# The end of a one-core decoder layer: feed-forward accumulators combined on VectorE in one block, and the residual added inside the output DMAs

## What is computed

```
mix = concat(latent_attention, sliding_window_attention) @ w_o
x1  = x + rms_norm(mix, g_mix_post)
h   = rms_norm(x1, g_ffn_pre)
ff  = (silu(h @ w_gate) * (h @ w_up)) @ w_down        # 2048 -> 5632 -> 2048
out = x1 + rms_norm(ff, g_ffn_post)
rms_norm(y, g) = y * rsqrt(mean(y*y) + 1e-6) * g
```

## Time and profile before

| | |
|---|---|
| median of 3 runs | 2082.83 us (2082.64 to 2082.87) |
| the profiled execution | 2083.53 us |
| its span in the trace | 2081.7 us |
| PE busy | 1998.4 us, 96% |
| DVE busy | 1114.0 us, 54% |
| ACT busy | 684.9 us, 33% |
| POOL busy | 113.6 us, 5% |
| granted PE clock, mean of the span | 0.986 of full speed |

### The profile page before, as it was taken

One profiled execution on the slowest core, in us unless ns is written; L12 is line 12 of the kernel. 1 busy time (PEld: TensorE's weight loads), 2 busy tenths in 40 slices (PEclk: granted clock), 3 DMA queues, 4 the chain that ended last, 5 costly groups with the idle time before them and its releaser, 6 DMA issues. The chain is left out here.

```text
span 2081.7 us, 21411 instructions
## 1 busy us (share of the span) xinstructions
PE 1998.4 (96%) x9062; PEld 1651.1 (79%) x9062; DVE 1114.0 (54%) x1278; ACT 684.9 (33%) x850; POOL 113.6 (5%) x64
## 2 busy tenths in 40 slices
PE   8999879999998999999999999999999999999994
PEld 6888667778886888888888888888888788888873
DVE  5753585563225433433334333343334788888887
ACT  5331463453226222222222222222222633333342
POOL 1200130000003000000000000000000000000034
PEclk9999999999998999999999999999999999999997
DMA  7433201115321554454444654445542756545633
GB/s 240 111 101 96 66 12 57 54 43 200 101 94 48 192 162 129 125 168 139 137 144 140 194 144 137 118 135 158 150 134 79 267 222 243 212 181 214 242 124 119
DMA packets 292058, 293.24 MB, mean 141 GB/s; under 512 B 4899, under 2 KB 228220, under 8 KB 286204
## 3 DMA queue, kind: packets, MB, share of 16 engines
q1 hardware_dynamic: 288928, 285.23, 43.1%
q10 hardware_dynamic: 3036, 6.66, 1.0%
HBM read 243.09 MB, written 51.93 MB: 142 GB/s over the span
## 5 line engine op out<-in xcount | busy, mean ns | idle before, releaser
L534 PE MATMUL pair<-act_hi,whi 128*128 128x512 f32 x1712 | 669.7, 391 | 0.0
L536 PE MATMUL pair<-act_hi,wlo 128*128 128x512 f32 x1712 | 666.5, 389 | 0.0
L535 PE MATMUL pair<-act_lo,whi 128*128 128x512 f32 x1712 | 666.3, 389 | 0.0
L425 DVE TENSOR_TENSOR wlo<-raw,whi 128x2048 fp32r<-128x2048 f32 x134 | 296.2, 2213 | 247.5 <-ACT whi L418 247.5
L534 PEld LDWEIGHTS pair<-act_hi,whi 128*128 128x128 f32 x1712 | 321.7, 188 | 67.0 <-issue 1.1
L536 PEld LDWEIGHTS pair<-act_hi,wlo 128*128 128x128 f32 x1712 | 321.5, 188 | 67.1
L535 PEld LDWEIGHTS pair<-act_lo,whi 128*128 128x128 f32 x1712 | 321.7, 188 | 66.1 <-issue 0.5
L418 ACT ACTIVATE whi<-raw 128x2048 fp32r<-128x2048 f32 x135 | 248.5, 1843 | 358.9 <-PE pair L536 338.3
L1979 PE MATMUL pair<-ring_hi,hfs 128*128 128x512 f32 x528 | 206.3, 391 | 4.6 <-DVE ring_lo L1500 4.6
L1981 PE MATMUL pair<-ring_hi,hfs 128*128 128x512 f32 x528 | 206.0, 390 | 0.0
L1980 PE MATMUL pair<-ring_lo,hfs 128*128 128x512 f32 x528 | 206.0, 390 | 0.0
(11 more groups left out here) (260 smaller groups left out, 2125.5 us busy)
## 6 DMA issues: line engine op xcount, KB each, us to landing
raw<-in_w_gate SPq DMA_DIRECT2D x44, 1024.0 KB, 5.5
raw<-in_w_up SPq DMA_DIRECT2D x44, 1024.0 KB, 5.7
w_b<-in_w_down SPq DMA_DIRECT2D x40, 1024.0 KB, 5.0
h_forms<-hst SPq DMA_DIRECT2D x22, 1792.0 KB, 7.3
hfs<-h_forms SPq DMA_DIRECT2D x30, 1024.0 KB, 7.7
raw<-in_w_in SPq DMA_DIRECT2D x19, 1024.0 KB, 5.7
raw<-in_w_o SPq DMA_DIRECT2D x16, 1024.0 KB, 4.9
xin<-in_x SPq DMA_DIRECT2D x4, 1024.0 KB, 11.2
```

The source lines that it names most:

```text
L425: last = nc.vector.tensor_tensor(dst, src, f(hi), ALU.subtract)
L534: nc.tensor.matmul(out_ap, a[0], b[0], start=first, stop=False)
L535: nc.tensor.matmul(out_ap, a[0], b[1], start=False, stop=False)
L536: return nc.tensor.matmul(out_ap, a[1], b[0], start=False, stop=last)
```

## The change

1. POOL's ten additions and DVE's four are gone from iterations 10 and 11. Instead DVE does all fourteen (`mix(0)`, `mix(1)`) directly behind the low part of P83, followed by the gain multiplications of cb 0, and only then the adds of P81 and P82.
2. x1 is written to the output tensor itself in place of `x1_dram`. It isn't read back.
3. y is scaled by rstd in place: by ACT for both halves of t = 0 and 1 and the right half of t = 3, by DVE (`y_normed`) for both halves of t = 2 and the left half of t = 3. POOL issues eight DMAs of 128 x 1024 that add y to what stands in the output (`accum_op=ALU.add`). SP issues no output DMA.
4. ACT's squares of iteration 10 move behind its last high part.

```diff
-                        sp_.dma_start(x1_dram[t], x1[:, t, :]).then_inc(x1_out, 16)
+                        sp_.dma_start(out_v[t], x1[:, t, :]).then_inc(x1_out, 16)
...
-                elif it + 1 == ITERS and f_ in (1, 3, 4, 5):
-                    sp_.wait_ge(d_lo, n + 1)
-                    t = (1, 3, 4, 5).index(f_)
-                    sp_.dma_start(x1_row[t][:, :], x1_dram[t]).then_inc(x1_in[t], 16)
...
-            for t in range(TB):
-                sp_.wait_ge(y_ready, t + 1)
-                w = shared(t).stop
-                sp_.dma_start(out_v[t][:, 0:1024], x1_row[t][:, 0:1024]).then_inc(y_out, 16)
...
-            sp_.wait_ge(y_out, 16 * (2 * TB + 1))
+            sp_.wait_ge(y_out, 16 * 2 * TB)
...
-            for it in (ITERS - 2, ITERS - 1):
-                cb = it % 2
-                before = 5 * (it - ITERS + 2)
-                pool.wait_ge(*evictions(7 * it))
-                add_into(5, 0, cb)
...
+            def add_to_out(t, half):
+                nc.gpsimd.dma_start(out_v[t][:, 1024 * half:1024 * half + 1024], y_part(t, half),
+                                    accum_op=ALU.add).then_inc(y_out, 16)
+
+            pool.wait_ge(x1_out, 16 * TB)
+            for t in (0, 1):
+                for half in (0, 1):
+                    pool.wait_ge(y_scaled, 2 * t + half + 1)
+                    add_to_out(t, half)
+            for half in (0, 1):
+                pool.wait_ge(y_ready, half + 1)
+                add_to_out(2, half)
+            pool.wait_ge(y_scaled, 5)
+            add_to_out(3, 1)
+            pool.wait_ge(y_ready, 3)
+            add_to_out(3, 0)
...
+                if n == PRODUCTS - 1:
+                    act.wait_ge(d_done, PRODUCTS - 7)
+                    for half, t0, done in ((0, 0, 1), (1, 0, 4), (0, 2, 6), (1, 2, 7)):
+                        act.wait_ge(y_mixed, done)
+                        y_square(t0, half, 0)
+                        y_square(t0 + 1, half, 0)
+                    act.wait_ge(y_mixed, 14)
+                    y_square(2, 1, 1)
+                    y_square(3, 1, 1)
+                if m in (PRODUCTS - 3, PRODUCTS - 2):
                     act.wait_ge(*evictions(m))
...
             root_of(0, 2, 8)
             act.wait_ge(*evictions(PRODUCTS - 1))
             y_square(2, 0, 1)
             act.wait_ge(rstd_ready, 4)
-            act.wait_ge(gained, 6)
-            y_times_rstd(0)
-            y_times_rstd(1)
+            act.wait_ge(gained, 7)
+            y_times_rstd(0, 0)
+            y_times_rstd(0, 1)
             root_of(2, 3, 9)
             act.wait_ge(d_added, evictions(PRODUCTS - 1)[1] + 1)
             y_square(3, 0, 1)
-            act.wait_ge(rstd_ready, 5)
-            y_times_rstd(2)
+            y_times_rstd(1, 0)
+            y_times_rstd(1, 1)
             root_of(3, 4, 10)
             act.wait_ge(rstd_ready, 6)
-            y_times_rstd(3)
+            y_times_rstd(3, 1)
...
-                if last_it >= 0 and f_ in (4, 5):
-                    dve.wait_ge(y_based, 5 * last_it + (4, 1)[f_ - 4])
-                if last_it >= 0 and f_ == 6:
-                    dve.wait_ge(y_mixed, 2 * last_it + 1)
+                if n in (PRODUCTS - 3, PRODUCTS - 2):
+                    dve.wait_ge(y_mixed, 14)
...
+            def mix(cb):
+
+                dve.wait_ge(*evictions(PRODUCTS - 8 if cb == 0 else PRODUCTS - 4))
+                for m, (dst, src, after) in enumerate(((5, 0, 0), (2, 0, 0), (1, 2, 2), (4, 1, 3), (6, 2, 3),
+                                                       (6, 3, 5), (3, 1, 6))):
+                    if after:
+                        dve.wait_ge(y_mixed, 7 * cb + after)
+                    nc.vector.tensor_tensor(y_of(dst, cb), y_of(dst, cb), y_of(src, cb), ALU.add).then_inc(y_mixed, 1)
...
-                if n == PRODUCTS:
+                if n == PRODUCTS - 1:
                     dve.wait_ge(g_row_in, 16)
-                    y_times_gain(2, 1, 0, 2)
+                    mix(0)
+                    mix(1)
+                    y_times_gain(0, 0, 0, 2)
+                    y_times_gain(0, 1, 0, 4)
+                    y_times_gain(2, 0, 0, 6)
+                    y_times_gain(2, 1, 0, 8)
...
+            def y_normed(t, half):
+                nc.vector.tensor_scalar(y_part(t, half), y_part(t, half), rstd[:, t:t + 1], None,
+                                        ALU.mult).then_inc(y_ready, 1)
...
             late_piece(2)
-            dve.wait_ge(gained, 7)
-            y_residual(0)
-            y_residual(1)
             y_rstd(2, 3, 15, 9, 5, lambda: late_gain(2))
             late_piece(3)
             dve.wait_ge(gained, 8)
-            y_residual(2)
+            y_normed(2, 0)
+            y_normed(2, 1)
             y_rstd(3, 4, 16, 10, 6, lambda: late_gain(3))
             dve.wait_ge(gained, 9)
-            y_residual(3)
+            y_normed(3, 0)
```

More of the change, by code:

```diff
@@ L248, in build @@
         h_forms = nc.dram_tensor("h_forms", (7, P, FF_PAIRS, 512), F32, kind="Internal").ap()
-        x1_dram = nc.dram_tensor("x1_dram", (TB, P, D), F32, kind="Internal").ap()
         x_in = [sem(f"x_in{c}") for c in range(4)]
@@ L271, in build @@
         s_norm = sem("s_norm")
-        y_pool = sem("y_pool")
         hi_ready = sem("hi_ready")
@@ L302, in build @@
         x1_out = sem("x1_out")
-        x1_in = [sem(f"x1_in{t}") for t in range(TB)]
-        y_based = sem("y_based")
         y_mixed = sem("y_mixed")
@@ L1083, in _ @@
                     product_copy(m)
[L1084 to L1089, removed]
+                if n == PRODUCTS - 1:
[8 more added lines that the diff above has]
+                if m in (PRODUCTS - 3, PRODUCTS - 2):
                     act.wait_ge(*evictions(m))
-                    half, t0 = ((1, 0), (0, 0), (0, 2))[m % 7 - 4]
-                    y_square(t0, half, cb)
-                    y_square(t0 + 1, half, cb)
+                    y_square(0, PRODUCTS - 2 - m, 1)
+                    y_square(1, PRODUCTS - 2 - m, 1)
             def root_of(t0, t1, n):
@@ L1097, in root_of, with y_times_rstd @@
                 nc.scalar.activation(root[:, t0:t1], mean[:, t0:t1], ACT.Sqrt).then_inc(root_done, 1)
-            def y_times_rstd(t):
-                a = y_part(t, 1)[:, shared(t)]
-                nc.scalar.activation(a, a, ACT.Copy, scale=rstd[:, t:t + 1]).then_inc(y_scaled, 1)
+            def y_times_rstd(t, half):
+                nc.scalar.activation(y_part(t, half), y_part(t, half), ACT.Copy,
+                                     scale=rstd[:, t:t + 1]).then_inc(y_scaled, 1)
             root_of(0, 2, 8)
@@ L1599, in y_rstd @@
                 dve.wait_ge(rstd_ready, n_rstd)
-            def y_residual(t):
-                dve.wait_ge(x1_in[t], 16)
-                parts = [(0, slice(0, 1024))]
-                if shared(t).stop < 1024:
-                    parts.append((1, slice(shared(t).stop, 1024)))
-                for half, a in parts:
-                    dst = x1_row[t][:, half * 1024 + a.start:half * 1024 + a.stop]
-                    last = nc.vector.scalar_tensor_tensor(out=dst, in0=y_part(t, half)[:, a], scalar=rstd[:, t:t + 1],
-                                                          in1=dst, op0=ALU.mult, op1=ALU.add)
-                last.then_inc(y_ready, 1)
+            def y_normed(t, half):
+                nc.vector.tensor_scalar(y_part(t, half), y_part(t, half), rstd[:, t:t + 1], None,
+                                        ALU.mult).then_inc(y_ready, 1)
             def late_piece(t):
                 dve.wait_ge(d_first if t == 2 else d_done, 1 if t == 2 else PRODUCTS)
-                dve.wait_ge(y_mixed, 3)
+                dve.wait_ge(y_mixed, 13)
                 a = y[6][:, t - 2, 512:1024]
```

31 lines of the change are left out of this document (removed).

## The result

| | before | after |
|---|---|---|
| device time, median of 5 | 2082.83 us (2082.39 to 2084.00) | 2103.51 us (2102.75 to 2104.72) |
| ratio | | 1.0099, interval 1.0084 to 1.0114 |
| span of the profiled execution | 2081.7 us | 2101.7 us |
| first reduction of the last stage | 2057.57 | 2057.54 |
| from there to the end of the span | 24.1 us | 44.2 us |

The change costs 20.7 us, where 4.8 were predicted with 2095 as the upper end. Slower is right, the size is not. The table says where to look: up to the first reduction the two programs take the same time, the arithmetic behind it ends 6.8 us earlier (6.5 were predicted), and all of the loss lies in what comes after the arithmetic.

What follows compares the result with a forecast made beforehand. The end was taken as bound by DVE and what it waits for, after the change by the DMA engines: 2062.7 + 1.2 + 21.6 + 1.0 = 2086.5 us of span, 2087.6 on the median. Range 2076.3 to 2095 us.

Steps and rivals of the forecast that it cites:

- Up to the low part of P83, and the fourteen additions: Before the last stage: low part done at 2031.4, additions on DVE 16.8 us, first reduction at 2057.7 against 2057.57.
- The last stage's arithmetic: From the first reduction to ACT's last scaling: ends at 2070.7, 6.5 us before the present end of 2077.19.
- The list of what is gone: Last stage: four instructions y * rstd + x1, two 2 us stalls beside POOL, and POOL's four additions vanish.
- The output DMAs: End of the kernel: eight adding DMAs become the bound, span ending at 2086.5, 4.8 us over before.
- the likeliest case: Output transfers: the second read costs a second pass, 2.4 to 3.2 us a DMA; chance 0.38.
- eight times 2.70 is 21.6: Output transfers: total us of DMA engine time for eight adding DMAs, whose pieces get ready within 8 us.
- for POOL I take 1.2: Start of the output DMAs: 1.2 us from POOL's issue to the first byte, against 0.8 for SP.
- The size of the pass: Output transfers: 2.70 us for each 512 KB adding DMA, against 1.35 for a plain one.
- POOL's issue: Output DMAs: each issue by POOL takes 1.0 us, against 0.34 for SP's.
- hidden: Output transfers: the second read costs nothing, 1.35 us a DMA, POOL's issues decide, 2077.1 us; chance 0.24.
- partly hidden: Output transfers: 1.8 to 2.3 us a DMA, 2082.0 us at 2.0; chance 0.21.
- passes that don't overlap at all: Output transfers: two reads and the write in turn, 4.05 us a DMA, 2098.4 us; with anything above 3.2, chance 0.17.

Runs made afterwards that it cites:

- its return at the other end: POOL's mixing of before, with DVE alone doing the output rows and SP issuing plain DMAs, against the kernel before: 2078.87 us, ratio 0.9982.
- the small DMA ahead: The kernel after plus one small plain DMA from POOL in the last iteration, to a buffer nobody reads: 2101.22 us, ratio 1.0083 to the kernel before.

## Why the prediction was wrong

- **Up to the low part of P83, and the fourteen additions**: right. The add of P80 at 2027.82 (2028.1 said), the low part done at 2031.2 (2031.4), the additions 16.98 (16.8), the first reduction at 2057.54 (2057.7). That the earlier end of PE buys nothing is shown by the mixing alone (1.0003) and by its return at the other end (0.9979 with it, 0.9982 without).
- **The last stage's arithmetic**: right, 2070.38 for 2070.7, with the first scaled piece 0.2 early and the wait for ACT's root in its place. The list of what is gone was too short: DVE had three stalls beside POOL in this stage and not two (the third is the gain of 2.58, 1.90 too long), and five instructions y * rstd + x1 and not four. The time was laid out instruction by instruction and doesn't hang on that list.
- **The output DMAs**: this is the step that failed, and all 15.2 us are in it. Its mechanism, that the DMA engines become the bound because a DMA that adds takes them about twice as long as a plain one, held as far as it went: 3.2 a DMA for 1.35, at the upper edge of the 2.4 to 3.2 of the likeliest case. That the forecast had the sign right is owed to this. But "eight times 2.70 is 21.6", added to one first byte, took two things for granted. First, that the DMAs follow each other without a gap. They wait for a ring that holds three, and the engines stand idle for 8.05 us; the ring size moves this as it should (last stage 53.0, 44.2 and 40.1 with one, three and four in flight). Nothing in the trace of before could show it, since POOL issued no DMA there; but the ring's size stands in the line that makes the program, and I did not ask how many DMAs of 128 rows it holds. Second, "for POOL I take 1.2" was taken as the whole of the start. With the small DMA ahead, issue to first byte is 1.5; in the kernel after the issue itself comes 2.85 us after the piece, and the first byte 1.7 to 1.9 behind the issue. Less the 0.2 by which the piece is early, that is about the 3.1. What delays the first issue stays open.
- **The size of the pass**: 2.70 was mis-sized by 0.5, 4.05 us in all. It was my estimate, twice the 1.35 of a plain DMA; that a second read is a whole second pass is shown by no run. What the runs show in its place is 2.66 for the add within SBUF at its start and 3.2 for the add into DRAM, 2.4 times a plain DMA.
- **POOL's issue**: 0.86 alone, 1.0 said, and it decides nothing, as the DMA engines are the bound. Three issues take 3.19 beside DVE's and ACT's scalings and 2.66 without them. Whether the scalings hold POOL up there was not tested; it would be worth 0.5, off the path. It does take longer than SP's, 0.86 for 0.34; that code on POOL does the work was my reason for the 1.0, and all that the page shows of it is the kind of the queue, software_dynamic for POOL's DMAs (q0) and hardware_dynamic for SP's (q1).
- **The rivals**: hidden and partly hidden fell with the 3.2; passes that don't overlap at all, 4.05, fell too, though their time (2098.4) was nearest. The text said that it would be wrong if the DMA engines idled between the output DMAs, and that is what they did, yet no rival had this as a mechanism, so the range ended at 2095.

## What to carry to other kernels

A DMA that adds in place is not a free adder: here it takes 2.4 times the DMA engines' time of a plain one (3.2 us for 1.35) and, by the estimate from the groups, about twice the ring's room (269 to 336 bytes for 129 to 146), and where POOL had done nothing for 1415 us the first issue came 2.8 to 3.7 us behind its piece in six kernels, 1.0 behind it in the one that adds within SBUF. If it pays at all it is for one early piece, whose transfer ends before most others are ready, and here even that gain (0.8 us of the median) isn't shown. Before moving several DMAs to POOL's queue, find out how many of them its ring holds, since past that number each group paid 2 to 4 us of idle DMA engines here. And where POOL helps VectorE and VectorE's instructions stretch beside it, try first whether VectorE alone is faster: here it was, by 4 us.

## What was not expected of the hardware

- An adding DMA of 512 KB from SBUF to DRAM: 3.2 us of all 16 engines, 1.35 for the plain one; within SBUF about 2.66. In DRAM the rate also swings, 137 to 187 GB/s by stretches of 3 us at a share of 0.93 or more, and single microseconds reach the 197 of SBUF (197 at 2069 and 2075, 209 at 2087): the 0.5 that DRAM costs would lie in the slow stretches. Why is open.
- POOL's issue: 0.53 us for the plain DMA, 0.86 for the adding one.
- With 1024 bytes of ring, adding DMAs went as 3, 3, 1, 1, where 3, 3, 2 would fit as well; with 1344 as 4, 4. What splits the last two, and why the whole group has to land before the next issue while adds within SBUF go on one by one, none of the runs tells.
